# Rotary queries projected once, their halves exchanged by two products with a constant matrix

## The reference

```
q = (_rmsnorm(cq, q_norm) @ w_q_up).reshape(B, S, MLA_HEADS, MLA_NOPE_DIM + MLA_ROPE_DIM)
q_rope = _apply_rope(q[..., MLA_NOPE_DIM:], cos[:, None, :], sin[:, None, :])
q_full = jnp.concatenate([q[..., :MLA_NOPE_DIM], q_rope], axis=-1)

def _apply_rope(x, cos, sin):
    x1, x2 = jnp.split(x.astype(jnp.float32), 2, axis=-1)
    return jnp.concatenate([x1 * cos - x2 * sin, x2 * cos + x1 * sin], axis=-1).astype(x.dtype)
```

## Time and profile before

| | us |
|---|---|
| median of 3 runs | 1768.68 (1767.65 to 1775.11) |
| profiled execution, time | 1769.71 |
| profiled execution, span of the core | 1767.6 |
| TensorE busy | 1685.2 (95%), 9399 products |
| VectorE busy | 773.6 (44%) |
| ScalarE busy | 770.0 (44%) |
| GpSimd busy | 607.2 (34%) |
| mean granted TensorE clock | 0.991 of full speed |

### The profile page before, as it was taken

One profiled execution on the slowest core, in us unless ns is written; L12 is line 12 of the kernel. 1 busy time (PEld: TensorE's weight loads), 2 busy tenths in 40 slices (PEclk: granted clock), 3 DMA queues, 4 the chain that ended last, 5 costly groups with the idle time before them and its releaser, 6 DMA issues.

```text
span 1767.6 us, 24369 instructions
## 1 busy us (share of the span) xinstructions
PE 1685.2 (95%) x9399; PEld 1365.1 (77%) x9399; DVE 773.6 (44%) x2029; ACT 770.0 (44%) x1565; POOL 607.2 (34%) x304
## 2 busy tenths in 40 slices
PE   6999999999999999999999999998899999999998
PEld 6777778887787877778777677877678888887876
DVE  1566636466264343325666627699514111000052
ACT  3455553466443535433456643424735222212242
POOL 4332223332333232233322222463224444443423
PEclk9999999999999999999999999999999999999999
DMA  5222225222543231243221234522143333233312
GB/s 153 60 55 50 60 94 162 84 64 66 143 142 88 60 84 49 66 149 108 66 42 46 60 138 123 148 77 72 48 143 96 96 100 101 96 96 95 119 60 83
DMA packets 215693, 161.16 MB, mean 91 GB/s; under 512 B 53723, under 2 KB 196859, under 8 KB 215580
## 3 DMA queue, kind: packets, MB, share of 16 engines
q1 hardware_dynamic: 205616, 130.21, 26.1%
q10 hardware_dynamic: 9660, 29.12, 5.2%
q0 software_dynamic: 304, 0.29, 0.2%
HBM read 148.32 MB, written 11.14 MB: 90 GB/s over the span
## 4 chain that ended last, share of the span: by engine, by line
PE 59%; DVE 9%; ACT 6%; POOL 3%; issue 2%; DMA 1%; ACTq 1%; POOLq 0%; DVEq 0%
PE banks L471 16%; PE banks L473 16%; PE banks L472 16%; PE banks L714 3%; PE banks L683 3%; PE banks L729 3%; POOL w_lo L2659 3%; ACT w_hi L1297 1%; ACT AB L1428 1%; DVE misc L2505 1%; ACT G L1548 1%; DVE misc L2492 1%; DVE top L2504 1%; ACT AB L1454 1%; PE banks L698 1%
## 5 line engine op out<-in xcount | busy, mean ns | idle before, releaser
L2659 POOL TENSOR_TENSOR w_lo<-w_raw,w_hi 128x1024 fp32r<-128x1024 f32 (+4 forms) x254 | 578.5, 2285 | 1132.1 <-ACT w_hi L1297 1131.7
L471 PE MATMUL banks<-XTh,w_hi 128*128 128x512 f32 (+4 forms) x1216 | 452.4, 372 | 16.6 <-POOL w_lo L2659 9.1
L473 PE MATMUL banks<-XTh,w_lo 128*128 128x512 f32 (+4 forms) x1216 | 445.9, 367 | 0.0
L472 PE MATMUL banks<-XTl,w_hi 128*128 128x512 f32 (+4 forms) x1216 | 445.9, 367 | 0.0
L1297 ACT ACTIVATE w_hi<-w_raw 128x1024 fp32r<-128x1024 f32 (+4 forms) x254 | 253.5, 1005 | 154.2 <-PE banks L473 81.9
L471 PEld LDWEIGHTS banks<-XTh,w_hi 128*128 128x128 f32 (+1 forms) x1216 | 229.6, 189 | 61.3 <-issue 15.3
L473 PEld LDWEIGHTS banks<-XTh,w_lo 128*128 128x128 f32 (+1 forms) x1216 | 229.5, 189 | 38.0
L472 PEld LDWEIGHTS banks<-XTl,w_hi 128*128 128x128 f32 (+1 forms) x1216 | 229.9, 189 | 36.4 <-issue 0.5
L471 PE MATMUL banks<-w_hi,OTh 128*128 128x512 f32 (+1 forms) x448 | 173.1, 386 | 7.8 <-POOL w_lo L2659 7.2
L473 PE MATMUL banks<-w_hi,OTl 128*128 128x512 f32 (+1 forms) x448 | 168.1, 375 | 0.0
L472 PE MATMUL banks<-w_lo,OTh 128*128 128x512 f32 (+1 forms) x448 | 168.0, 375 | 0.0
(11 more groups left out here) (196 smaller groups left out, 2373.2 us busy)
## 6 DMA issues: line engine op xcount, KB each, us to landing
w_raw<-in_w_gate_up_dram SPq DMA_DIRECT2D x44, 512.0 KB, 3.8
w_raw<-in_fox_w_in_dram SPq DMA_DIRECT2D x30, 512.0 KB, 4.1
w_raw<-in_mla_w_in_dram SPq DMA_DIRECT2D x26, 512.0 KB, 4.3
w_raw<-in_w_in_dram SPq DMA_DIRECT2D x24, 512.0 KB, 3.8
w_raw<-in_w_down_dram SPq DMA_DIRECT2D x22, 512.0 KB, 3.5
w_raw<-in_swa_w_in_dram SPq DMA_DIRECT2D x20, 512.0 KB, 3.8
w_raw<-in_mla_w_out_dram SPq DMA_DIRECT2D x16, 512.0 KB, 3.7
x_spill<-AB ACTq DMA_DIRECT2D x16, 512.0 KB, 2.9
```

Source lines behind the costliest of these rows:

```text
L471: nc.tensor.matmul(o, ah, bh, start=first, stop=False, skip_group_check=True)
L472: nc.tensor.matmul(o, ah, bl, start=False, stop=False, skip_group_check=True)
L473: return nc.tensor.matmul(o, al, bh, start=False, stop=last, skip_group_check=True)
L2659: pool.tensor_tensor(view(w_lo, u, RING), view(w_raw, u, RAW), view(w_hi, u, RING).bitcast(F32), ALU.subtract).then_inc(lo_done, 1)
```

## The change

The unit q_rope has 128 columns instead of 256, and GpSimd copies nothing. TensorE makes one group of nine products for it. ScalarE and VectorE take its high and low part into the rope slots of QKh and QKl. After the keys TensorE multiplies both parts with a constant 0/1 matrix, which exchanges the halves of 16, into a group of its own; VectorE multiplies that with SIN and goes on as before, now behind the keys' low parts. The matrix is made from the identity by two copies on ScalarE at the start. The first rope bank is no longer given back by the product with COS but by the subtraction of the low part.

```diff
--- before.py
+++ after.py
@@ -102,8 +102,8 @@
                                                for x in range(2)], 0))
 
         def rope(g):
-            units.append(("q_rope", QR // P, 2 * P, [(None, ROPE * n, ROPE, reads(wq, (4 * g + h) * QH + HD, (4 * g + h + 1) * QH))
-                                                     for n, h in enumerate((0, 2, 1, 3))], 1))
+            units.append(("q_rope", QR // P, P, [(None, ROPE * n, ROPE, reads(wq, (4 * g + h) * QH + HD, (4 * g + h + 1) * QH))
+                                                 for n, h in enumerate((0, 2, 1, 3))], 0))
 
         def keys_values(g):
             loads = []
@@ -229,6 +229,7 @@
         w_raw = sb("w_raw", [P, RAW, UNIT])
         w_hi, w_lo = sb("w_hi", [P, RING, UNIT], F32R), sb("w_lo", [P, RING, UNIT], F32R)
         ident = sb("ident", [P, P])
+        swap_halves = sb("swap_halves", [P, P], F32R)
         zmask = sb("zmask", [P, S])
         ones = sb("ones", [P, P])
         otmp = sb("otmp", [P, S])
@@ -300,6 +301,7 @@
             sem(n) for n in ("win_in", "tri_in", "pool_in", "p_in", "rel_in", "onehot_in", "rel_dma"))
         aug_in = [sem(f"aug_in{p}") for p in range(4)]
         ident_in = sem("ident_in")
+        swap_made = sem("swap_made")
         ln_var = sem("ln_var")
         own = sem("own")
         chain = sem("chain")
@@ -907,22 +909,27 @@
                     ready_q[c.pair + p] = c.g
                     weave()
 
+                rope_at = {}
+
                 def rope(g):
                     h, l = unit("q_rope")
-                    for half in range(2):
-                        o = begin()
-                        hs = slice(half * P, half * P + P)
-                        for k in range(3):
-                            mm = three(o[:, :], h[:, k, hs], l[:, k, hs], OTh[:, k, :], OTl[:, k, :], k == 0, k == 2)
-                            if k < 2:
-                                weave()
-                        end(mm)
-                        if half == 0:
-                            weave()
+                    o = begin()
+                    for k in range(3):
+                        mm = three(o[:, :], h[:, k, :], l[:, k, :], OTh[:, k, :], OTl[:, k, :], k == 0, k == 2)
+                    end(mm)
                     released()
+                    rope_at[g] = c.g
                     for p in range(2):
                         ready_rope[c.pair + 2 * g + p] = 8 * j + 2 * g + p + 1
-                    weave()
+
+                def swapped(g):
+                    pe.wait_ge(swap_made, 2)
+                    groups_stored(pe, rope_at[g])
+                    o = begin()
+                    for n, rows in enumerate((QKh, QKl)):
+                        mm = nc.tensor.matmul(o[:, :], swap_halves[:, :], rows[:, 5 + g % 2, :], start=n == 0, stop=n == 1,
+                                              skip_group_check=True)
+                    end(mm)
 
                 kv = []
 
@@ -958,6 +965,7 @@
                             query(0)
                             pe.wait_ge(c_lo, 5 * j + 5)
                             keys(0)
+                            swapped(0)
                             vals(0)
                             query(1)
                             pe.wait_ge(kr_done, 7 * (j + 1))
@@ -970,6 +978,7 @@
                                 tile("gate")
                         elif pos == 2:
                             keys(g)
+                            swapped(g)
                         elif pos == 3:
                             vals(g)
                     elif pos == 1 and i < 7:
@@ -1652,7 +1661,10 @@
 
                 def rope(g):
                     advance()
-                    c.g += 2
+                    from_tmp(QKh[:, 5 + g % 2, :], group()[:, :])
+
+                def rotated(g):
+                    c.g += 1
                     from_tmp(QKh[:, 5 + g % 2, :], RA)
                     hi(QKl[:, 5 + g % 2, :], RA)
 
@@ -1671,6 +1683,7 @@
                             rope(0)
                             query(0)
                             keys(0)
+                            rotated(0)
                             vals(0)
                             query(1)
                     elif i % 2 and i < 5:
@@ -1683,6 +1696,7 @@
                                 gate(2)
                         elif pos == 2:
                             keys(g)
+                            rotated(g)
                         elif pos == 3:
                             vals(g)
                     elif pos == 1 and i < 7:
@@ -1706,6 +1720,10 @@
                     split(0)
                     split(1)
             split(2)
+            act.wait_ge(ident_in, 16)
+            for x in range(2):
+                dst, src = (v[:, :].rearrange("p (g s n) -> p g s n", g=4, s=2) for v in (swap_halves, ident))
+                nc.scalar.activation(dst[:, :, x, :], src[:, :, 1 - x, :], ACT.Copy).then_inc(swap_made, 1)
             act.wait_ge(pool_cst, 2)
             rope_tables(0)
             mla(0)
@@ -2328,8 +2346,14 @@
                     stored(lo(QKl[:, 3 + p % 2, :], o[:, :], QKh[:, 3 + p % 2, :]))
 
                 def rope(g):
-                    rotate_first(P, 0)
-                    rope_rest(g)
+                    o = group()
+                    nc.vector.tensor_tensor(RA, o[:, :], COS, ALU.mult).then_inc(g_tmp, 1)
+                    rope_banks.append(o)
+
+                def rope_low(g):
+                    stored(lo(QKl[:, 5 + g % 2, :], rope_banks.pop()[:, :], QKh[:, 5 + g % 2, :]))
+
+                rope_banks = []
 
                 def rope_rest(g):
                     rotate_rest(P, 0)
@@ -2356,8 +2380,10 @@
                     if i == -2:
                         if pos == 0:
                             rope(0)
+                            rope_low(0)
                             query(0)
                             keys(0)
+                            rope_rest(0)
                             low_rope(0, 1)
                             c.g += 2
                             query(1)
@@ -2366,15 +2392,16 @@
                     elif i % 2 and i < 5:
                         g = (i + 3) // 2
                         if pos == 4:
-                            rotate_first(P, 0)
+                            rope(g)
                         elif pos == 1:
-                            rope_rest(g)
+                            rope_low(g)
                             query(i + 3)
                             if i < 0:
                                 gate(2)
                                 gate_at[2] = c.g
                         elif pos == 2:
                             keys(g)
+                            rope_rest(g)
                         elif pos == 3:
                             low_rope(g, 1)
                             c.g += 2
```

## The result

The changed kernel takes 1782.03 us (median of 5 runs, 1777.77 to 1785.95) against 1768.68 before: 1.0066 of the time, with a 95% interval of 1.0048 to 1.0083. That is slower by more than the measurement's 0.5%, 9 us above the forecast, and 2 us above the range. The profiled execution has a span of 1780.2 us against 1767.6, so 12.6 us are to be found.

A forecast was written before the change was run, and what follows sets the result against it. TensorE, busy 95%, was taken to bound the kernel, but moved waits to outweigh its 12.7 us of saved products: +2.3 us over two layers and +1.7 for group 0's clock, +4.0 on 1768.7, gave 1772.7 us; range 1758 to 1780.

The forecast's parts named there:

- What bounds the kernel, and the products: TensorE, busy 95%, bounds the kernel; seven fewer products in each of 8 rope groups give 12.7 us if nothing waits.
- Groups 2 and 3, the pause: TensorE idles about 3.9 us before the keys, half clock follows; +0.3 us for each of the two groups.
- T: Start of `swapped` in group 2: 149.9 at full clock, 150.6 at half; values' second half at T+6.05.
- Group 3: Taken to look like group 2, with the same pause of about 3.9 us and +0.3 us.
- Group 1: New wait of 1.6 us before the gate, whose bank is freed after `norm` and rope_low; values +0.75 us.
- Group 0: TensorE pauses from 78.1 to 80.4 before the keys; values -0.2 to 0, or +1.5 us if the clock falls.
- the edge: Group 0's pause is borderline for making the clock fall, so counted in one of two layers: +1.7 us.
- The sum: Groups 0 to 3 give -0.2, +0.75, +0.3, +0.3: +1.15 us a layer; two layers +2.3, group 0's clock +1.7: +4.0.
- (C): Clock also falls behind the pauses of groups 0 and 1, 1.7 us each per layer: 1777.8 us; chance 0.20.
- Its addition for a longer fall in groups 2 and 3: A second clock fall behind the pauses before the keys adds up to 0.6 us a group: 1780.2 us.
- (A): The saving arrives whole, rounding and subtraction coming before TensorE wants the bank: 1756.0 us; chance 0.12.
- (B): The saving arrives in part, clock holding in groups 2 and 3: 1766.7 us, down to 1762; chance 0.19.

## Why the prediction was wrong, by its own steps

**What bounds the kernel, and the products.** Right in kind: 56 fewer products, none of them visible in the time. The run without the second projection shows how right: about 3 us of 14.5, since the two engines behind TensorE had no room at that place. The averages of 44% said the opposite, and the replay of the queues was right to set them aside. The step that failed is the price of the chains behind the swap, group by group: a layer was to lose 1.15 us, and it lost 5.96. The terms follow, one by one.

**Groups 2 and 3, the pause.** Forecast 3.9 us before the keys, measured 3.73 and 3.76, with the half clock behind both and the old 2.33 us wait gone. The chain behind the swap was mis-sized. Forecast T = 150.6; the swap came at 152.80, which is 150.75 when the 2.05 us that groups 0 and 1 brought are taken off. That it fits is in part luck: I had the swap wait for the first key half's low part, and it waited for nothing. TensorE issued the second key half up to 152.57, at half clock for the most part, and the low part was in by then (151.86 + 0.69). From there I put SIN at T + 0.7 and it came at T + 1.51. The rows of 153.00 and 153.70 show why: the second key half's rounding and low part stand ahead of SIN on VectorE, and I had counted the first half alone. With T + 6.83 for the values' second half in place of T + 6.05, and 0.15 for T, group 2 comes to +1.25 in place of +0.3, which is what was measured.

**Group 3** was taken for a copy of group 2, and it isn't one: +1.96 with the same pause and the same chain. Its stretch at half clock lasts twice as long (8 us at 0.57, with the swap itself at 196.08 still slow), and from the keys to the swap it takes 5.26 us, against 4.41 in group 2. Why the stretch lasts longer there is not settled.

**Group 1.** +0.75 forecast, +1.27 measured. The new wait before the gate is there, 1.52 of 1.6, and so is that of 1 us before the swap, 1.11. The profile names another engine for the first one, GpSimd with the low part of the gate's weights:

```profile
101.94 2.38 POOL L2686 TENSOR_TENSOR w_lo<-w_raw,w_hi 128x1024 fp32r<-128x1024 f32 x1 [8.97 <-ACT w_hi L1306]
```
```profile
101.15 2.41 POOL L2659 TENSOR_TENSOR w_lo<-w_raw,w_hi 128x1024 fp32r<-128x1024 f32 x1 [8.76 <-ACT w_hi L1297]
```

The second line is the kernel before. There this low part is done at 103.56 and the second rope projection hides it, since the gate starts at 103.92; it comes 0.79 later after the change, because the whole group does, and now TensorE stands waiting for it. I had named no such queue. It costs little, for the rope bank itself comes back only at about 104.2 (VectorE's low part starts at 103.52), so the gate at 104.35 is 0.1 late against the forecast, once the 0.78 is taken off. The swap is 0.3 late and the values 0.5, and the 0.2 between them is the swap's own: its two products took 0.63 us behind the wait, and 0.45 was counted.

**Group 0.** The pause of 2.26 us was forecast (2.3), and so was the price if the clock falls: +1.5, measured +1.48. I called it the edge and counted it in one layer of two; in the execution profiled for the result it came in both, which is 1.7 us in the sum. In the other profiled execution of the same kernel it came in one, and that one took 3.6 us less. On which side of the edge an execution falls, no row tells.

**The sum.** A layer 5.96 against 1.15 (2.0 with half of the clock's price): 1.7 for group 0's clock, 0.5 in group 1, 0.9 and 1.7 in groups 2 and 3. Twice 5.96 is 11.9, and the whole is 12.6; the other stretches nearly cancel: -0.7 ahead of the first layer, -1.7 between the layers, +3.0 behind the fourth. There the half clock of 1107 to 1114 takes up to 0.45 x 7 = 3.2 us. No row of before spoke of it.

**The rivals.** (C) had the right mechanism for group 0 and the slow side, with 0.20; it said 1777.8 to 1780.2. Its addition for a longer fall in groups 2 and 3 came in group 3. It was wrong on group 1: its pause of 1.5 us was followed by no half clock. The Trainium skill, "TensorE: Matmul & The Clock Gate", section "HAM oscillation — how this bites in real kernels", warns of just this, bursts that start slow behind pauses; the trace agrees for 2.26, 3.73 and 3.76 us, not for 1.52. (A) and (B) are out by the time alone, and the run that keeps both orders and leaves the second projection out gained 3 us and not 14.5. What decided was none of the engines' shares but the order: with `swapped` ahead of the keys and no bank held behind the exponentials, the changed kernel goes from 1.0075 to 0.9986 of the time before, and with spare banks for group 0 as well to 0.9929.

**What stays open.** The half-clock stretches far behind the change. The profiled executions of the change in its new order, without and with spare banks, differ by 13.4 us of span. Of these 8.5 are there by the end of layer 4, the greater part by the spare banks themselves; the last 4.9 fall in the second block, where the one without spare banks runs 1093 to 1099 at half clock and the other doesn't. Nor do the pauses there explain it: in the second block both the kernel before (1094 to 1100) and the changed one (1104 to 1110) keep TensorE busy for only about half of 6 us, and just the latter loses its clock. For that reason the share of the 25.6 us that is owed to the products, to the order and to the clock can't be given in figures either. Nor was the kernel before given spare banks, or an order fitted to its own two rope groups and its copies; so it is not shown that the change is what makes 0.9929 possible.

## What to carry to other kernels

Before you price products taken from a busy engine, look at what the next ones wait for: leave the work out in one kernel and read the waits, and if the same instruction starts at the same time, the engine behind it sets the time there, and the saving is worth little until its order changes. When one result is to serve as the source of another (here a rounding, a low part and a swap in place of a second projection), the bank is held by the slowest reader's queue; write down what stands in that queue, in full, for every engine, second halves included. And where a new pause is as long as one behind which this trace already shows half clock, count that at every such place, in addition to the wait.

## What the runs showed of the hardware

In the first layer of the kernel before and of the changed one, half clock followed each of TensorE's waits of 2.26 us or more and none of 1.52 or less; in layer 4 one wait of 2.26 us was followed by it in one execution of the changed kernel and not in the other. The reordered kernels have waits of 2.0 us before `mix` and show both: the granted clock fell to 0.58 and 0.61 over 4 us behind the two of the one without spare banks, and of the two of the other it fell behind the first alone (its rows, 148 to 153 and 188 to 194; columns as above):

```profile
148.00:153.00 5.00, 4.94 (x24) 3.07 (x25) 2.98 (x11) 0.00 (x0) 0.00 (x0) 0.66 0.75 188
188.00:194.00 6.00, 5.84 (x46) 4.60 (x47) 4.96 (x13) 0.97 (x2) 0.61 (x1) 1.00 0.55 180
```

How long it lasted differed too: 4 us at 0.57 behind 3.73 us, 8 us at 0.57 behind 3.76 us.

VectorE's addition of two SBUF tiles, 0.69 us, took 2.27 in the kernel with the new order and no spare banks, where it started 0.70 us into a GpSimd subtraction of 2.41 us:

```profile
145.80 2.27 DVE L2008 TENSOR_TENSOR AB<-AB,G 128x512 f32<-128x512 f32 x1
```
```profile
145.10 2.41 POOL L2697 TENSOR_TENSOR w_lo<-w_raw,w_hi 128x1024 fp32r<-128x1024 f32 x1 [12.43 <-ACT w_hi L1306]
```

At 145.80 the subtraction has 1.7 us to go, and 1.58 is what the addition took too long: it seems to have stood until the subtraction was through. All six such additions of groups 1 to 3 in the two layers took 2.27 to 2.56 us in this trace, so this is a price of the new order, and no run gives it apart. The Trainium skill, "SBUF — State Buffer", section "Who interferes with whom", says that a VectorE instruction with both inputs in SBUF contends with a GpSimd instruction that reads SBUF, over a port pair that is locked for one of them at a time; these two rows agree. No run was made for it alone.
